# The gate products of a two-layer hybrid block: twelve weight tiles per layer as six folded pairs

## Chip, cores and metric
One core of a Trainium2 chip. The metric is the device time of one execution in microseconds (us); lower is better.

## The reference, cut to what matters
The model has 512 tokens, width 2048 and two layers. The stage that is changed is the last line of the loop, the product `x @ ple_gate_w[i]` (2048 x 2048) and the sigmoid gate around it:

```python
for i in range(DEPTH):                    # DEPTH = 2
    y = _even_layer(x, ...) if i % 2 == 0 else _conv_layer(x, ...)
    x = _layernorm(DEEPNORM_ALPHA * x + y, post_ln_g[i], post_ln_b[i])
    x = x + (p[i] @ ple_w[i]) * jax.nn.sigmoid(x @ ple_gate_w[i])
```

## The kernel before, in words
All activations stand transposed: 16 chunks (`KC`) of 128 channels by 512 tokens (`T`). `Y` holds x, `Z` holds the product `p @ ple_w`. A matrix product is made in three passes for precision: each operand is split into a rounded part and a rest (`a_hi`, `a_lo` for activations, `w_hi`, `w_lo` for weights), and TensorE adds hi x hi, hi x lo and lo x hi. A weight tile is 128 x 2048: 16 blocks of 128 x 128, which make one chunk of 128 output channels. So a tile costs 16 x 3 = 48 matmuls of 512 columns. All matmuls have one line, the helper `mm` (L745).

A tile passes through five hands. SyncE loads it into one of the two slots of `w_raw` (in `whole`, L519) when the slot's last tile has been split. ScalarE writes `w_hi` (`split`, L1231) once TensorE has finished the tile that used that slot before. VectorE writes `w_lo` as `w_raw` minus `w_hi` (`split`, L1705). TensorE multiplies (`gemm`), into the PSUM banks `G[0]` and `G[1]` in turn. ScalarE applies the sigmoid from the bank (L1592), VectorE multiplies by `Z` (L2368) and adds to `Y` (L2370), and GpSimd stores the finished chunk to DRAM (`store`, L659).

The gate stage of a layer (`W_GATE`, tiles 0 to 15) stands behind the layer norm. In that norm VectorE subtracts the mean (L2118) and multiplies by the deviation (L2122), ScalarE applies scale and bias (L1577) and makes `a_hi` of the chunk (L1235), and GpSimd makes `a_lo` (`x1_low`, L651). Tiles 0 and 1 run interleaved while those chunks arrive (`gemm_pair`, with tile 1 seven chunks behind), tiles 2 to 14 run one after another in `gemms` and `gemm`, and tile 15 is made in quarters (layer 0, where ScalarE and VectorE split the new x as its chunks pass) or by halves of the tokens (layer 1). In layer 0 the convolution's first two tiles follow, interleaved in the same way.

The output projection of each layer (`W_OUT`) already has a folded form, `folded_pair`: two tiles make a block of two by two with 6 chunk pairs, and the four block products of each pair of chunks and half of the tokens, eight in all, are replaced by seven from sums of weights (`t1` to `t4`) and sums of activations (`folds`). Its pieces are split at L1484 (ScalarE) and L2194 (VectorE), its sums of weights are made by DMAs that add, from GpSimd's queue (L626, L629), its sums of activations at L2159, L2162 and L2164 with the split at L1474 and L2185 (VectorE's first one of a fold also serves L2175), and its extra products are emptied from PSUM by L2203 and L2212 to L2222. Its piece of 6 chunks has 18 matmuls of 256 columns; the 4 chunks outside of the scheme are done as before, with 512 columns. Each engine runs its list in the order in which it is written; waits are on semaphores.

## Time and profile before

| | us |
|---|---|
| median of 3 runs | 2089.8 |
| lowest, highest | 2089.51, 2090.85 |
| the profiled execution, its own time | 2089.52 |
| its span (first to last instruction) | 2087.8 |
| TensorE matmul busy in the span | 2080.8 (100%) |
| VectorE, ScalarE, GpSimd busy | 1341.0, 872.9, 394.8 |
| chain that ended last: share of TensorE | 97% |
| mean granted TensorE clock | 1.000 |

A row of instructions gives line, engine, operation, what is written and read with partitions x elements, the count, then busy us and the mean ns of one, then the idle time of the engine just before and what ended it. Back-to-back instructions of one engine overlap by some tens of ns in the records, so the distance of two starts is what an instruction costs in a full queue. GpSimd is POOL, VectorE DVE, ScalarE ACT, TensorE PE.

### The profile page before, as it was taken

Reading aid. Unit: us, or ns where it says so; the run is one execution under the profiler, and the core shown is the slowest. Engines: PE = TensorE matmul, PEld = TensorE weight load, DVE = VectorE, ACT = ScalarE, POOL = GpSimd, SP = SyncE. Lnnn points to the kernel's source line nnn. Section 1 sums busy time; section 2 is a strip of 40 time slices with the busy share of each in tenths; the row PEclk is TensorE's granted clock in tenths of the full one; section 3 lists DMA queues with packets and bytes.
Section 4 is the critical chain, followed back from the end, with each engine's and each line's share of the span. In section 5 each row is a group of like instructions: output and inputs, shape, how many; then the busy total and the mean of one; then the engine's idle time right before and its main releaser. Section 6 shows DMA issues by size and latency. Waiting matters only on the chain.

```text
span 2087.8 us, 29899 instructions
## 1 busy us (share of the span) xinstructions
PE 2080.8 (100%) x11050; PEld 1749.4 (84%) x11050; DVE 1341.0 (64%) x2295; ACT 872.9 (42%) x1148; POOL 394.8 (19%) x232
## 2 busy tenths in 40 slices
PE   9999999999999999999999999999999999999999
PEld 7878888888888888898788888888888888997888
DVE  5235575665765747787733588888888986887332
ACT  4225465464654657354622322222323453447221
POOL 0000000000000004110400034444757521104000
PEclk9999999999999999999999999999999999999999
DMA  8322222212222122695333322222222235852431
GB/s 320 142 101 90 73 80 80 76 64 81 67 95 80 60 80 81 161 228 145 107 109 121 136 100 85 98 101 101 91 91 101 101 121 127 218 158 82 145 108 68
DMA packets 46947, 233.51 MB, mean 112 GB/s; under 512 B 5456, under 2 KB 5728, under 8 KB 26896
## 3 DMA queue, kind: packets, MB, share of 16 engines
q1 hardware_dynamic: 35424, 190.33, 26.4%
q0 software_dynamic: 10000, 36.36, 7.0%
q10 hardware_dynamic: 1440, 5.77, 0.9%
q8 instruction: 45, 0.74, 0.1%
q14 instruction: 38, 0.31, 0.0%
HBM read 224.05 MB, written 8.39 MB: 111 GB/s over the span
## 4 chain that ended last, share of the span: by engine, by line
PE 97%; DMA 1%; DVE 1%; ACT 1%; issue 0%; DVEq 0%; ACTq 0%
PE G L745 83%; PE X L745 8%; PE T L745 5%; DMA w_raw<-wall_in 1%; PE T L927 1%; DVE w_lo L2194 0%; PE T L1048 0%; ACT w_hi L1484 0%; ACT a_hi L1235 0%; ACT Z L1430 0%; ACT Y L1577 0%; PE T L1053 0%; PE T L899 0%; DVE Y L2229 0%; ACT L1322 0%
## 5 line engine op out<-in xcount | busy, mean ns | idle before, releaser
L745 PE MATMUL G<-a_hi,w_hi 128*128 128x512 f32 (+1 forms) x2524 | 980.0, 388 | 0.7 <-ACT a_hi L1235 0.6
L745 PE MATMUL G<-a_hi,w_lo 128*128 128x512 f32 (+1 forms) x2524 | 974.0, 386 | 0.0
L745 PE MATMUL G<-a_lo,w_hi 128*128 128x512 f32 (+1 forms) x2524 | 972.3, 386 | 0.0
L1231 ACT ACTIVATE w_hi<-w_raw 128x2048 fp32r<-128x2048 f32 x147 | 281.7, 1916 | 787.3 <-PE G L745 774.2
L1705 DVE TENSOR_TENSOR w_lo<-w_raw,w_hi 128x2048 fp32r<-128x2048 f32 x104 | 242.0, 2327 | 494.2 <-ACT w_hi L1231 494.2
L745 PEld LDWEIGHTS G<-a_hi,w_hi 128*128 128x128 f32 x2524 | 474.1, 188 | 99.4 <-ACT a_hi L1235 1.5
L745 PEld LDWEIGHTS G<-a_hi,w_lo 128*128 128x128 f32 x2524 | 474.1, 188 | 96.2 <-issue 0.2
L745 PEld LDWEIGHTS G<-a_lo,w_hi 128*128 128x128 f32 x2524 | 474.2, 188 | 94.5 <-issue 0.5
L2429 DVE SCALAR_TENSOR_TENSOR T<-tmp,par,T 128x512 f32<-128x512 f32 x464 | 306.9, 747 | 0.0
L687 POOL TENSOR_TENSOR w_lo<-w_raw,w_hi 128x2048 fp32r<-128x2048 f32 x45 | 207.8, 4618 | 232.4 <-ACT w_hi L1231 232.4
L1484 ACT ACTIVATE w_hi<-w_raw 128x768 fp32r<-128x768 f32 (+1 forms) x86 | 66.2, 783 | 89.7 <-PE G L745 27.1
L2194 DVE TENSOR_TENSOR w_lo<-w_raw,w_hi 128x768 fp32r<-128x768 f32 (+1 forms) x86 | 73.7, 880 | 38.3 <-ACT w_hi L1484 37.8
L671 POOL TENSOR_TENSOR a_lo<-Y,a_hi 128x512 fp32r<-128x512 f32 x15 | 21.3, 1456 | 339.6 <-DVE Z L1917 339.6
L666 POOL CAST v_lo<-Y 128x512 fp32r<-128x512 f32 x1 | 0.6, 609 | 385.3 <-PE X L745 385.3
L745 PE MATMUL T<-folds,w_hi 128*128 128x256 f32 x360 | 65.4, 283 | 0.0
L651 POOL TENSOR_TENSOR a_lo<-Y,a_hi 128x512 fp32r<-128x512 f32 x32 | 44.2, 1403 | 108.7 <-ACT a_hi L1235 108.4
L745 PEld LDWEIGHTS T<-folds,w_hi 128*128 128x128 f32 x360 | 56.4, 192 | 0.2
L745 PE MATMUL T<-folds,w_lo 128*128 128x256 f32 x180 | 50.9, 283 | 0.0
L2417 DVE TENSOR_TENSOR tmp<-G,tmp 128x512 f32<-128x512 f32 x16 | 11.0, 687 | 59.6 <-PE G L745 59.6
L1235 ACT ACTIVATE a_hi<-Y 128x512 fp32r<-128x512 f32 x80 | 46.0, 622 | 5.1 <-PE G L745 2.6
L1330 ACT ACTIVATE Z<-Z,nmx 128x128 f32<-128x128 f32 (+1 forms) x64 | 35.2, 552 | 20.8 <-DVE nmx L1990 20.7
L745 PE MATMUL G<-pk,w_hi 128*128 128x512 f32 x128 | 42.6, 413 | 0.5 <-ACT Z L1430 0.5
(336 smaller groups left out, 2246.9 us busy)
## 6 DMA issues: line engine op xcount, KB each, us to landing
w_raw<-wall_in SPq DMA_DIRECT2D x150, 1024.0 KB, 4.8
w_raw<-wall_in SPq DMA_DIRECT2D x42, 384.0 KB, 5.2
w_raw<-wall_in SPq DMA_DIRECT2D x36, 256.0 KB, 5.4
w_raw<-wall_in POOLq DMA_DIRECT2D x24, 384.0 KB, 5.5
Y<-w_in POOLq DMA_DIRECT2D x2, 2048.0 KB, 15.6
x_residual<-Y POOLq DMA_DIRECT2D x16, 256.0 KB, 3.7
out<-Y POOLq DMA_DIRECT2D x15, 256.0 KB, 3.6
Z<-xT_in SPq DMA_DIRECT2D x6, 512.0 KB, 9.4
```

The lines of the kernel that those rows point to most:

```text
L651: pool.tensor_tensor(a_lo[:, j, :], chunk(Y, j), a_hi[:, j, :].bitcast(F), ALU.subtract).then_inc(S("ops_split"), 1)
L671: pool.tensor_tensor(a_lo[:, c, :], chunk(Y, c), a_hi[:, c, :].bitcast(F), ALU.subtract).then_inc(S("ops_split"), 1)
L687: pool.tensor_tensor(w_lo[:, w.slot, :], w_raw[:, w.slot, :], w_hi[:, w.slot, :].bitcast(F), ALU.subtract).then_inc(S("w_split"), 1)
L745: return pe.matmul(o, l, r, start=start, stop=stop)
L927: last = pe.transpose(TB[at // T][:, at % T:at % T + P], prob_of(ti)[:, mj * P:(mj + 1) * P], ident)
L1231: f(w_hi[:, w.slot, :], w_raw[:, w.slot, :], ACT.Copy).then_inc(S("w_hi"), 1)
L1235: f(a_hi[:, j, :], chunk(Y, j), ACT.Copy).then_inc(S("ops_hi"), 1)
L1330: f(prob_of(ti), prob_of(ti), ACT.Exp, bias=nmx[:, o + ti:o + ti + 1], accum_out=rsum[:, o + ti:o + ti + 1]).then_inc(S("exps"), 1)
L1484: f(w_ring[0][ring_slot(p, name)][:, 0:piece_width(name)], source(p, name), ACT.Copy).then_inc(S("w_hi" if last else "piece_hi"), KC - 2 * ...
L1705: tt(w_lo[:, w.slot, :], w_raw[:, w.slot, :], w_hi[:, w.slot, :].bitcast(F), ALU.subtract).then_inc(S("w_split"), 1)
L2194: tt(w_ring[1][at][:, 0:n], source(p, name), w_ring[0][at][:, 0:n].bitcast(F), ALU.subtract).then_inc(S("w_split" if last else "piece_low" ...
L2429: stt(acc, src, cw, acc, op0=ALU.mult, op1=ALU.add).then_inc(S("tap"), 1)
```

## The change
Tiles 2 to 13 of each gate stage become six pairs. In a pair, chunks 0 to 2 and 3 to 5 are the two halves of the scheme (`GATE_K` = 3 chunk pairs) and chunks 6 to 15 are done as before: `r1` and `r2` are those ten blocks of the first and of the second tile (1280 wide, 512 columns), and `b11, t1, t3, t2, b22, b21, t4` are seven products of 3 blocks (384 wide, 256 columns). Tile 14 is done plainly from three pieces, tile 15 as before.

- Sums of weights: VectorE adds them (`add_weights`), in place or into `gate_sum` (in `tmp`).
- Sums of activations: VectorE makes three folds (`make_fold`) behind its last instruction of the layer norm, ScalarE and VectorE split them (`gate_fold_high`, `gate_fold_low`), and only then is the first piece of pair 1 split.
- `w_hi` and `w_lo` hold `r1`, `r2` and a ring of four places of 384; a piece is written when TensorE has done the fourth one before it.
- The products in `TB[0]`, `TB[1]` are emptied into `gate_pre` (the sum before the sigmoid, in `tmp`) in three steps between the last pieces' splits; the banks `X[1], X[2]` or `G[1], G[0]` are added behind (`add_bank`), and both chunks' sigmoids follow (`gate_sigmoid`).
- SyncE loads four pieces per pair in place of two tiles (640 KB and 384 KB of each tile). GpSimd's list is unchanged but for semaphore values.

The helpers that are left out below give semaphore values and places. The diff, with 12 spaces of indentation and empty lines taken out:

```diff
+GATE_K = 3
+GATE_QUAD = GATE_K * P
+GATE_REST = 2 * GATE_QUAD
+GATE_PAIRS = 6
+GATE_SMALL = ("b11", "t1", "t3", "t2", "b22", "b21", "t4")
+GATE_TILE = GATE_PAIRS + 1
+GATE_DONE = [(p, name) for p in range(1, GATE_TILE) for name in ("r1", "r2") + GATE_SMALL] + [
+    (GATE_TILE, name) for name in ("r1", "b11", "b21")]
+GATE_MADE = [(1, "r1")]
+for pair in range(1, GATE_TILE):
+    GATE_MADE += [(pair, name) for name in ("r2",) + GATE_SMALL[:4]] + [(pair + 1, "r1")]
+    GATE_MADE += [(pair, name) for name in GATE_SMALL[4:]]
+GATE_MADE += [(GATE_TILE, "b11"), (GATE_TILE, "b21")]
+N_GATE = len(GATE_MADE) - 1
+PIECES_BEFORE = (N_PIECES - 1, 2 * (N_PIECES - 1) + N_GATE)
...
+def gate_pieces(layer):
+    def load(p, tile, small):
+        at = slice(0, GATE_REST) if small else slice(GATE_REST, D)
+        sp.dma_start(w_raw[:, 1 - tile, at], wall[W_GATE[layer] + 2 * p + tile][:, at]).then_inc(
+            S(("b11_landed", "b22_landed")[tile] if small else "rest_landed"), 16)
+    sp.wait_ge(S("w_split"), W_GATE[layer] + 1)
+    load(1, 0, False)
+    load(1, 0, True)
+    sp.wait_ge(S("w_split"), W_GATE[layer] + 2)
+    load(1, 1, False)
+    load(1, 1, True)
+    for p in range(2, GATE_TILE + 1):
+        sp.wait_ge(*gate_low(layer, p - 1, "r1"))
+        load(p, 0, False)
+        if p < GATE_TILE:
+            sp.wait_ge(*gate_low(layer, p - 1, "r2"))
+            load(p, 1, False)
+            sp.wait_ge(*gate_low(layer, p - 1, "b22"))
+            load(p, 1, True)
+            sp.wait_ge(*gate_low(layer, p - 1, "b21"))
+            load(p, 0, True)
+    sp.wait_ge(*gate_low(layer, GATE_PAIRS, "b22"))
+    tile = W_GATE[layer] + KC - 1
+    sp.dma_start(w_raw[:, 0, :], wall[tile]).then_inc(S("w_landed0"), 16)
+    sp.wait_ge(*gate_low(layer, GATE_PAIRS, "b21"))
+    load(GATE_TILE, 0, True)
...
+def gate_products(layer, p, name, out, highs, lows, start, stop):
+    pe.wait_ge(*gate_low(layer, p, name))
+    hi, lo = gate_place(p, name)
+    n = len(highs)
+    for k in range(n):
+        at = slice(k * P, (k + 1) * P)
+        mm(out, hi[:, at], highs[k], start and k == 0, False)
+        mm(out, hi[:, at], lows[k], False, False)
+        last = mm(out, lo[:, at], highs[k], False, stop and k == n - 1)
+    return last
+def gate_pair(layer, p):
+    g = G_GATE[layer] + 2 * p
+    one, two = (X[1], X[2]) if p % 2 else (G[1], G[0])
+    first, second = TB[0][:, 0:HALF_T], TB[1]
+    if p > 1:
+        pe.wait_ge(*drained(Idx(g - 4)))
+        pe.wait_ge(*drained(Idx(g - 3)))
+    def tokens(chunks, half):
+        at = slice(half * HALF_T, (half + 1) * HALF_T)
+        return [a_hi[:, c, at] for c in chunks], [a_lo[:, c, at] for c in chunks]
+    def fold(s):
+        return [[gate_folds[k][:, s, n, :] for k in range(GATE_K)] for n in range(2)]
+    rest = range(2 * GATE_K, KC)
+    whole = [a_hi[:, c, :] for c in rest], [a_lo[:, c, :] for c in rest]
+    ones_at, twos_at = range(GATE_K), range(GATE_K, 2 * GATE_K)
+    done = S("piece_done")
+    gate_products(layer, p, "r1", one[:, :], *whole, True, False).then_inc(done, 1)
+    gate_products(layer, p, "r2", two[:, :], *whole, True, False).then_inc(done, 1)
+    if p > 1:
+        pe.wait_ge(*gate_emptied(layer, p - 1, 4))
+    else:
+        pe.wait_ge(S("fold_lo"), gate_fold(layer, GATE_K))
+    gate_products(layer, p, "b11", first, *tokens(ones_at, 0), True, True).then_inc(done, 1)
+    gate_products(layer, p, "t1", second[:, HALF_T:T], *fold(1), True, True).then_inc(done, 1)
+    gate_products(layer, p, "t3", second[:, 0:HALF_T], *fold(0), True, True).then_inc(done, 1)
+    pe.wait_ge(*gate_emptied(layer, p, 1))
+    gate_products(layer, p, "t2", first, *fold(2), True, True).then_inc(done, 1)
+    gate_products(layer, p, "b22", two[:, 0:HALF_T], *fold(3), False, True).then_inc(done, 1)
+    gate_products(layer, p, "b21", one[:, 0:HALF_T], *tokens(twos_at, 0), False, False).then_inc(done, 1)
+    gate_products(layer, p, "t4", one[:, HALF_T:T], *tokens(twos_at, 1), False, True).then_inc(
+        *((S("gemm_done"), 2 * GATE_PAIRS) if p == GATE_PAIRS else (done, 1)))
+def gate_tile(layer):
+    p, done = GATE_TILE, S("piece_done")
+    pe.wait_ge(*drained(Idx(G_GATE[layer] + 2 * p - 4)))
+    def whole(lo, hi):
+        return [a_hi[:, c, :] for c in range(lo, hi)], [a_lo[:, c, :] for c in range(lo, hi)]
+    gate_products(layer, p, "r1", X[1][:, :], *whole(2 * GATE_K, KC), True, False).then_inc(done, 1)
+    gate_products(layer, p, "b11", X[1][:, :], *whole(0, GATE_K), False, False).then_inc(done, 2)
+    gate_products(layer, p, "b21", X[1][:, :], *whole(GATE_K, 2 * GATE_K), False, True).then_inc(S("gemm_done"), 1)
...
-    gemms(w + 2, g + 2, KC - 4)
-    gemm(Idx(w + KC - 2), Idx(g + KC - 2))
+    for p in range(1, GATE_TILE):
+        gate_pair(layer, p)
+    gate_tile(layer)
...
+    def gate_fold_high(i):
+        act.wait_ge(S("fold_raw"), gate_fold(layer, i + 1))
+        if i == 2:
+            act.wait_ge(S("gemm_done"), W_PLE[layer][1] + 1)
+        f(gate_folds[i][:, :, 0, :], (gate_raw[1] if i else gate_raw[0]), ACT.Copy).then_inc(S("fold_hi"), 1)
+    def gate_piece_high(p, name):
+        if name[0] == "t":
+            act.wait_ge(*gate_after("centred", layer, 4 * (p - 1) + ("t1", "t3", "t2", "t4").index(name) + 1))
+        else:
+            act.wait_ge(*gate_landed(layer, p, name))
+        act.wait_ge(*gate_place_free(layer, p, name))
+        last = (p, name) == GATE_MADE[-1]
+        f(gate_place(p, name)[0], gate_source(p, name), ACT.Copy).then_inc(
+            S("w_hi" if last else "piece_hi"), 2 * GATE_PAIRS + 1 if last else 1)
+    def gate_sigmoid(p):
+        for n in range(2):
+            act.wait_ge(*drained(Idx(g + 2 * p + n)))
+            pre = gate_pre[:, n * T:(n + 1) * T]
+            f(pre, pre, ACT.Sigmoid).then_inc(S("squared"), 1)
+    for i in range(GATE_K):
+        gate_fold_high(i)
+    gate_piece_high(1, "r1")
+    gate(Idx(w), Idx(g), 0)
+    gate_piece_high(1, "r2")
+    gate(Idx(w + 1), Idx(g + 1), 0)
+    for p, name in GATE_MADE[2:]:
+        if name == "b11" and p > 1:
+            gate_sigmoid(p - 1)
+        gate_piece_high(p, name)
     gate_end = W_GATE[layer] + KC
+    split(Idx(gate_end - 1))
+    act.wait_ge(S("x_out"), KC * layer + KC - 2)
+    act.wait_ge(S("gemm_done"), gate_end - 1)
+    frees(f(ln_sq[1], X[1][:, :], ACT.Sigmoid), Idx(g + KC - 2))
...
-    with dve.Fori(0, KC // 2 - 1) as i:
-        for k in range(2):
-            split(Idx(w + 2 + k, 2, i))
-            gate(Idx(g + k, 2, i), i * 2 + k, i * 2 + (layer * KC + k + 1))
+    def make_fold(i):
+        n = gate_fold(layer, i)
+        dve.wait_ge(S("x1_ready"), layer * KC + GATE_K + i + 1)
+        if i == 2:
+            dve.wait_ge(S("fold_lo"), n)
+        raw = gate_raw[1] if i else gate_raw[0]
+        tt(raw[:, 0:2, :], Y4[:, i, :, :], Y4[:, i:GATE_K + i + 1:GATE_K, 1, :], ALU.subtract).then_inc(S("fold_step"), 1)
+        dve.wait_ge(S("fold_step"), 2 * n + 1)
+        tt(raw[:, 2, :], raw[:, 1, :], Y4[:, i, 0, :], ALU.subtract).then_inc(S("fold_step"), 1)
+        dve.wait_ge(S("fold_step"), 2 * n + 2)
+        tt(raw[:, 3, :], raw[:, 2, :], Y4[:, GATE_K + i, 0, :], ALU.add).then_inc(S("fold_raw"), 1)
+    def gate_fold_low(i):
+        dve.wait_ge(S("fold_hi"), gate_fold(layer, i + 1))
+        dve.wait_ge(S("fold_raw"), gate_fold(layer, i + 1))
+        tt(gate_folds[i][:, :, 1, :], (gate_raw[1] if i else gate_raw[0]), gate_folds[i][:, :, 0, :].bitcast(F),
+           ALU.subtract).then_inc(S("fold_lo"), 1)
+    def add_weights(p, name, dst, a, b):
+        dve.wait_ge(*gate_landed(layer, p, "b11"))
+        dve.wait_ge(*gate_landed(layer, p, "b22"))
+        n = 4 * (p - 1) + ("t1", "t3", "t2", "t4").index(name)
+        dve.wait_ge(*gate_after("centred", layer, n))
+        tt(dst, a, b, ALU.add).then_inc(S("centred"), 1)
+    def gate_piece_low(p, name):
+        dve.wait_ge(*gate_high(layer, p, name))
+        hi, lo = gate_place(p, name)
+        last = (p, name) == GATE_MADE[-1]
+        tt(lo, gate_source(p, name), hi.bitcast(F), ALU.subtract).then_inc(
+            S("w_split" if last else "piece_low"), 2 * GATE_PAIRS + 1 if last else 1)
+    def gate_lows(p, *names):
+        for name in names:
+            gate_piece_low(p, name)
+    one_right, two_left, two_right = [gate_pre[:, n * HALF_T:(n + 1) * HALF_T] for n in range(1, 4)]
+    def empty_one(p):
+        dve.wait_ge(*gate_done(layer, p, "b11"))
+        dve.tensor_copy(gate_pre[:, 0:HALF_T], TB[0][:, 0:HALF_T]).then_inc(S("fold_emptied"), 1)
+    def empty_two(p):
+        dve.wait_ge(*gate_done(layer, p, "t3"))
+        dve.tensor_copy(gate_pre[:, HALF_T:3 * HALF_T], TB[1][:, :]).then_inc(S("fold_emptied"), 1)
+        dve.wait_ge(*gate_emptied(layer, p, 2))
+        tt(two_right, two_left, TB[1][:, 0:HALF_T], ALU.subtract).then_inc(S("fold_emptied"), 1)
+    def empty_three(p):
+        dve.wait_ge(*gate_done(layer, p, "t2"))
+        dve.wait_ge(*gate_emptied(layer, p, 3))
+        tt(fold_sum, gate_pre[:, 0:HALF_T], TB[0][:, 0:HALF_T], ALU.add).then_inc(S("fold_emptied"), 1)
+        dve.wait_ge(*gate_emptied(layer, p, 4))
+        tt(one_right, one_right, fold_sum, ALU.add).then_inc(S("fold_emptied"), 1)
+        two = gate_pre[:, T:2 * T].rearrange("p (h t) -> p h t", h=2)
+        tt(two, two, fold_sum.unsqueeze(1).broadcast_to([P, 2, HALF_T]), ALU.subtract).then_inc(S("fold_emptied"), 1)
+        dve.wait_ge(*gate_emptied(layer, p, 6))
+    def add_bank(p, n):
+        dve.wait_ge(*gate_done(layer, p, ("t4", "b22")[n]))
+        bank = ((X[1], X[2]) if p % 2 else (G[1], G[0]))[n]
+        pre = gate_pre[:, n * T:(n + 1) * T]
+        frees(tt(pre, pre, bank[:, :], ALU.add), Idx(g + 2 * p + n))
+    def gate_two(p):
+        for n in range(2):
+            j = 2 * p + n
+            dve.wait_ge(*gate_after("squared", layer, 2 * (p - 1) + n + 1))
+            pre = gate_pre[:, n * T:(n + 1) * T]
+            tt(pre, pre, chunk(Z, j), ALU.mult).then_inc(S("ple_gated"), 1)
+            dve.wait_ge(S("ple_gated"), layer * KC + j + 1)
+            tt(chunk(Y, j), chunk(Y, j), pre, ALU.add).then_inc(S("x_out"), 1)
+    make_fold(0)
+    make_fold(1)
+    gate_fold_low(0)
+    gate_fold_low(1)
+    make_fold(2)
+    gate_fold_low(2)
+    for p in range(1, GATE_TILE):
+        b12, b22, b21 = [gate_source(p, name) for name in ("t3", "b22", "b21")]
+        if p == 1:
+            gate_lows(p, "r1")
+            gate(Idx(g), 0, layer * KC + 1)
+            gate_lows(p, "r2")
+            gate(Idx(g + 1), 1, layer * KC + 2)
+        else:
+            add_bank(p - 1, 0)
+            gate_lows(p, "r2")
+            gate_two(p - 1)
+        add_weights(p, "t1", gate_sum, gate_source(p, "b11"), b12)
+        add_weights(p, "t3", b12, b12, b22)
+        gate_lows(p, "b11", "t1")
+        add_weights(p, "t2", gate_sum, gate_sum, b22)
+        gate_lows(p, "t3", "t2")
+        add_weights(p, "t4", gate_sum, gate_sum, b21)
+        gate_lows(p + 1, "r1")
+        empty_one(p)
+        gate_lows(p, "b22")
+        empty_two(p)
+        gate_lows(p, "b21")
+        empty_three(p)
+        gate_lows(p, "t4")
+        add_bank(p, 1)
+    add_bank(GATE_PAIRS, 0)
+    gate_lows(GATE_TILE, "b11", "b21")
+    gate_two(GATE_PAIRS)
+    split(Idx(w + KC - 1))
     if w + KC < W_TILES:
         split(Idx(w + KC))
-    gate(Idx(g + KC - 2), KC - 2, layer * KC + KC - 1)
+    bank = Idx(g + KC - 2)
+    dve.wait_ge(*drained(bank))
+    tt(ln_sq[1], ln_sq[1], chunk(Z, KC - 2), ALU.mult).then_inc(S("ple_gated"), 1)
+    dve.wait_ge(S("ple_gated"), layer * KC + KC - 1)
+    tt(chunk(Y, KC - 2), chunk(Y, KC - 2), ln_sq[1], ALU.add).then_inc(S("x_out"), 1)
     if layer == 0:
         for j in range(12):
             low(OPS_CONV, j, chunk(Y, j))
```

## Rows read from the trace of the kernel before

**Rows 1.** The page: busy time by engine, then two stretches of 10.88 and 20.58 us.

```profile
PE 2080.8 (100%) x11050; PEld 1749.4 (84%) x11050; DVE 1341.0 (64%) x2295; ACT 872.9 (42%) x1148; POOL 394.8 (19%) x232
...
1046.09:1056.97 10.88, 10.88 (x49) 9.01 (x48) 3.58 (x3) 2.40 (x2) 0.54 (x1) 1.00 0.37 120
902.72:923.30 20.58, 20.58 (x152) 19.62 (x151) 19.60 (x31) 11.29 (x15) 3.41 (x4) 1.00 0.94 233
```

**Rows 2.** Timeline, all engines, where an output pair's `b11` ends (start us, us, engine).

```profile
910.18 0.40 PE L745 MATMUL T<-folds,w_hi 128*128 128x256 f32 x2
910.38 0.42 DVE L2203 COPY fold_sum<-T 128x256 f32<-128x256 f32 x1 [0.26 <-PE T L745]
```

**Rows 3.** Timeline of VectorE, emptying an output pair's products.

```profile
920.39 0.41 DVE L2219 TENSOR_TENSOR fold_sum<-fold_sum,T 128x256 f32<-128x256 f32 x1
920.84 0.42 DVE L2221 TENSOR_TENSOR Y<-Y,fold_sum 128x256 f32<-128x256 f32 x1
921.18 0.68 DVE L2222 TENSOR_TENSOR Y<-Y,fold_sum 128x512 f32<-128x512 f32 x1
921.97 0.69 DVE L2229 TENSOR_TENSOR Y<-Y,X 128x512 f32<-128x512 f32 x1
```

**Rows 4.** Timeline of VectorE, start of a fold in layer 0.

```profile
855.40 0.69 DVE L2159 TENSOR_TENSOR tmp<-Y 128x512 f32<-128x512 f32 x1
856.13 0.42 DVE L2162 TENSOR_TENSOR tmp<-tmp,Y 128x256 f32<-128x256 f32 x1
```

**Rows 5.** Groups by form: splits of 768 weights, of folds (VectorE and ScalarE).

```profile
L2194 DVE TENSOR_TENSOR w_lo<-w_raw,w_hi 128x768 fp32r<-128x768 f32 x62 | 58.4, 954 | 34.2 <-ACT w_hi L1484 34.1
L2185 DVE TENSOR_TENSOR folds<-tmp,folds 128x1024 fp32r<-128x1024 f32 x12 | 14.6, 1219 | 0.0
L1474 ACT ACTIVATE folds<-tmp 128x1024 fp32r<-128x1024 f32 x12 | 12.7, 1056 | 21.9 <-DVE tmp L2164 21.9
```

**Rows 6.** Timeline, all engines, where TensorE waited for a piece's `w_lo`.

```profile
876.08 0.96 DVE L2194 TENSOR_TENSOR w_lo<-w_raw,w_hi 128x768 fp32r<-128x768 f32 x1 [2.21 <-ACT w_hi L1484]
...
876.63 0.28 PE L745 MATMUL X<-folds,w_lo 128*128 128x256 f32 x1
...
877.09 0.39 PE L745 MATMUL X<-a_hi,w_hi 128*128 128x256 f32 x1 [0.19 <-DVE w_lo L2194]
877.32 0.28 PE L745 MATMUL X<-a_lo,w_hi 128*128 128x256 f32 x1
```

**Rows 7.** Timelines, start of the gate stage, layer 0: VectorE, ScalarE, GpSimd, TensorE.

```profile
1021.59 1.87 DVE L2122 TENSOR_TENSOR Y<-Y,X 128x512 f32<-128x512 f32 x3
...
1025.57 1.14 ACT L1235 ACTIVATE a_hi<-Y 128x512 fp32r<-128x512 f32 x2
...
1020.13 8.81 POOL L651 TENSOR_TENSOR a_lo<-Y,a_hi 128x512 fp32r<-128x512 f32 x7 [0.58 <-ACT a_hi L1235]
...
1028.87 0.63 PE L745 MATMUL G<-a_lo,w_hi 128*128 128x512 f32 x2
1035.01 0.39 PE L745 MATMUL G<-a_hi,w_hi 128*128 128x512 f32 x1
```

**Rows 8.** Timelines of GpSimd and of VectorE, convolution stage.

```profile
1660.11 4.62 POOL L687 TENSOR_TENSOR w_lo<-w_raw,w_hi 128x2048 fp32r<-128x2048 f32 x1 [4.34 <-ACT w_hi L1231]
...
1661.24 4.03 DVE L2475 TENSOR_TENSOR Y<-Y,Z 128x512 f32<-128x512 f32 x1 [0.27 <-ACT Y L1684]
```

**Rows 9.** Timelines of GpSimd (two of 15 alike, here one) and of VectorE, output stage.

```profile
819.48 3.33 POOL L671 TENSOR_TENSOR a_lo<-Y,a_hi 128x512 fp32r<-128x512 f32 x1
...
818.26 3.40 DVE L1705 TENSOR_TENSOR w_lo<-w_raw,w_hi 128x2048 fp32r<-128x2048 f32 x1 [2.19 <-ACT w_hi L1231]
```

**Rows 10.** Timelines, convolution's first tiles: VectorE's split of the second, TensorE.

```profile
1190.75 2.28 DVE L1705 TENSOR_TENSOR w_lo<-w_raw,w_hi 128x2048 fp32r<-128x2048 f32 x1
...
1193.23 0.39 PE L745 MATMUL G<-a_hi,w_hi 128*128 128x512 f32 x1
```

**Rows 11.** The page: DMA issues, KB each and median us to landing.

```profile
w_raw<-wall_in SPq DMA_DIRECT2D x42, 384.0 KB, 5.2
```

More of the change, by code:

```diff
@@ L415, in landed @@
             in_pieces = (FOLD_TO + 1 - FOLD_FROM) * len([n for n in W_OUT if w.base > n + 2 * FOLD_TO])
+            in_pieces += (GATE_TILE if w.slot else GATE_PAIRS) * len([n for n in W_GATE if w.base > n + 2 * GATE_TILE])
             return S(f"w_landed{w.slot}"), w.half(1 - in_pieces) * 16
@@ L475, in after, with gate_after, gate_high @@
         def after(name, n, steps):
-            return S(name), steps + LN_COUNTS[name] * n
+            return S(name), steps + LN_COUNTS[name] * n + (GATE_COUNTS.get(name, 0) if n else 0)
+        def gate_after(name, layer, steps):
+            return S(name), steps + LN_COUNTS[name] * (2 * layer + 1) + GATE_COUNTS[name] * layer
+        def gate_high(layer, p, name):
+            n = GATE_MADE.index((p, name)) + 1
+            if n == len(GATE_MADE):
+                return S("w_hi"), W_GATE[layer] + 2 * GATE_TILE + 1
+            return S("piece_hi"), PIECES_BEFORE[layer] + n
@@ new lines, in gate_width, with gate_place @@
+        def gate_width(name):
+            return D - GATE_REST if name[0] == "r" else GATE_QUAD
+        def gate_place(p, name):
+            if name[0] == "r":
+                at = D if name == "r1" else 0
+            elif p == GATE_TILE:
+                at = GATE_RING[("b11", "b21").index(name)]
+            else:
+                at = GATE_RING[(7 * (p - 1) + GATE_SMALL.index(name)) % 4]
+            return [w.rearrange("p s n -> p (s n)")[:, at:at + gate_width(name)] for w in (w_hi, w_lo)]
@@ new lines, in gate_place_free @@
+        def gate_place_free(layer, p, name):
+            if name[0] == "r":
+                return gate_done(layer, p - 1, name) if p > 1 else (S("gemm_done"), W_GATE[layer] + int(name[1]))
+            if p == GATE_TILE:
+                return gate_done(layer, p - 1, {"b11": "b21", "b21": "t4"}[name])
+            n = 7 * (p - 1) + GATE_SMALL.index(name) - 4
+            if n < 0:
+                return S("gemm_done"), W_GATE[layer] + (1 if n < -2 else 2)
+            return gate_done(layer, n // 7 + 1, GATE_SMALL[n % 7])
@@ new lines, in gate_source, with gate_landed @@
+        def gate_source(p, name):
+            if name[0] == "r":
+                return w_raw[:, 1 if name == "r1" else 0, GATE_REST:D]
+            if name in ("t1", "t2", "t4"):
+                return gate_sum
+            slot, at = {"b11": (1, 0), "b21": (1, GATE_QUAD), "t3": (0, 0), "b22": (0, GATE_QUAD)}[name]
+            return w_raw[:, slot, at:at + GATE_QUAD]
+        def gate_landed(layer, p, name):
+            if name[0] == "r":
+                n = (2 * (N_FOLDS + 1) + 2 * GATE_PAIRS + 1) * layer + 2 * (N_FOLDS + 1) + min(2 * p, 2 * GATE_PAIRS + 1)
+                return S("rest_landed"), 16 * n
+            if name in ("b12", "b22", "t3"):
+                return S("b22_landed"), 16 * ((N_FOLDS + 1) * (layer + 1) + GATE_PAIRS * layer + p)
+            return S("b11_landed"), 16 * ((N_FOLDS + 1) * (layer + 1) + GATE_TILE * layer + p)
@@ L479, in quarter, with gate_emptied, gate_fold @@
+        def gate_emptied(layer, p, step):
+            return S("fold_emptied"), 8 * N_FOLDS * (layer + 1) + 6 * (GATE_PAIRS * layer + p - 1) + step
+        def gate_fold(layer, i):
+            return PAIR_K * (layer + 1) + GATE_K * layer + i
         def quarter(q):
@@ L1594, in second_part @@
                 w, g = W_GATE[layer], G_GATE[layer]
-                for j in range(2):
-                    split(Idx(w + j + 2))
-                    gate(Idx(w + j), Idx(g + j), 0)
-                with act.Fori(1, KC // 2 - 1) as i:
-                    for k in range(2):
-                        split(Idx(w + 2 + k, 2, i))
-                        gate(Idx(w + k, 2, i), Idx(g + k, 2, i), i * 2 + (k - 1))
+                def gate_fold_high(i):
[3 more added lines that the diff above has]
+                    f(gate_folds[i][:, :, 0, :], (gate_raw[1] if i else gate_raw[0]), ACT.Copy).then_inc(S("fold_hi"), 1)
@@ L2154, in fold @@
                         dve.wait_ge(S("gated"), second + 1)
[L2155 removed]
+                    n = layer * (PAIR_K + GATE_K) + i
                     if i >= 2:
```

52 lines of the change are left out of this document (35 added, 17 removed).

## The prediction

> **What bounds the kernel now.** First the busy times on the profile's page: TensorE is busy for 2080.8 us of a span of 2087.8, VectorE for 1341.0 [rows 1]. So only two things can move the end: what TensorE itself is given to do, and any wait that is put in front of it. Then two stretches of that section. A plain gate tile takes 10.88 us for 48 matmuls of 512 columns, all of it TensorE, with VectorE busy for 3.58: 0.2267 us per matmul, and 21.76 us per two tiles. A folded pair of the output projection takes 20.58 us for 24 matmuls of 512 columns and 126 of 256; taking off 24 x 0.2267 leaves 0.120 per matmul of 256 columns, a little over half. In that pair VectorE is busy for 19.60 of 20.58 us and still hides [rows 1].
>
> **What TensorE gets.** Per pair and pass set, r1 and r2 keep 10 blocks each: 60 matmuls x 0.2267 = 13.60 us. The seven products have 7 x 9 = 63 matmuls x 0.120 = 7.56 us, 1.08 per product. Together 21.16 against 21.76: 0.60 us saved per pair, 7.2 us in twelve pairs, if nothing waits. Tile 14 in three pieces still has 48 wide matmuls, 10.88 us. The gain per pair is small because six chunks give up 36 wide matmuls (8.16 us) for 7.56.
>
> **The tail of each pair.** The pieces are short: VectorE must now empty three products and split three weight pieces while TensorE runs b11 to b21, 1.08 us each. I count from the end of b11; then t3 ends at 2.16, t2 at 3.24, and TensorE wants b22 at 3.24, b21 at 4.32, t4 at 5.40. Prices: VectorE starts 0.20 after a product's end (910.18 to 910.38) [rows 2]. One start to the next costs 0.34 at 256 columns, 0.44 if it waits for the one before, and 0.79 behind a 512-wide one that is waited for [rows 3]; 0.73 by the fold's first step [rows 4]. A split of 384 has no row: between 256 (0.42 busy) [rows 3] and 768 (0.95) [rows 5] a line gives 0.555 busy, 0.47 start to start; the ends of the interval would shift the result by at most 0.13 each way per split. TensorE starts 0.05 after the split's end, 1.01 after its start at 768 [rows 6], so 0.61 after its start at 384, and the first matmuls behind a wait cost 0.10 more (the second starts 0.23 after the first, not 0.12) [rows 6].
> The list: empty_one at 0.20; b22's split by 0.9, in time. empty_two waits for t3: copy at 2.36, the subtraction at 3.09, b21's split at 3.43, ready at 4.04, in time by 0.28. empty_three then stands in front of t4's split: 3.90, 4.34, 4.68 and, since it waits for its own last result, t4's split only at 5.47. TensorE gets t4 at 6.08, 0.68 late, and with 0.10 for the restart a pair loses 0.78. So it costs 21.94 us: **0.60 saved, 0.78 lost, +0.17 us per pair, +2.0 for twelve.** Behind t4 nobody else waits for it: add_bank, r2's split, two gates (2.8 us), four sums of weights and five splits take VectorE to about 18.6, and the next b11 ends at 21.94, so the delay does not pile up. Those sums and splits cost nothing as long as these 3 us are left; if that cover goes, each 0.47 us is 0.47 us of TensorE.
>
> **Loads.** Each pair has four loads for two. The pieces b11 and b21 of the next pair are asked for at about 4.0, when b21 is split; such a load lands in 5.2 us [rows 11], at 9.3, and VectorE first adds them at 12.2. SyncE's wait for b22 and b21 stands in front of the loads of the next r1 and r2, wanted only at 17. At the end tile 15's megabyte is asked for ahead of tile 14's b11, which is wanted 14 us behind. GpSimd only stores here, two chunks at a time. I cost these at nothing.
>
> **The start of each gate stage**, twice. Before, VectorE ends the layer norm at 1023.39 (1021.59 and three steps of 0.60), ScalarE makes the last a_hi by 1026.71, and TensorE goes from tiles 0, 1 to tile 2 at 1035.01 [rows 7]. Now three folds stand between the norm and the first piece. Alone, a fold is 0.73 + 0.46 + 0.34 = 1.5 us [rows 3, 4], its high part 1.06 on ScalarE and its low part 1.22 [rows 5]. The third reuses the second's place, so it runs in series: low parts of the first two from 1027.8 to 1030.1, third fold to 1031.7, its high to 1032.8, its low to 1034.0. r1's high runs beside that (1280 wide, about 1.3, above the 1.06 for 1024), and its low (0.95 + 512 columns at 1.04 ns, the slope of that line, = 1.48) ends at 1035.6: TensorE starts 0.64 late, 0.74 with the restart.
> But GpSimd makes a_lo of chunks 9 to 15 in this very time, seven of 1.26 us in a row from 1020.13 to 1028.94 [rows 7]. Two rows show what that does. A VectorE product of two SBUF tensors, of 0.68 us otherwise, took 4.03 from 1661.24 and ended at 1665.27, 0.54 behind a GpSimd split that ended at 1664.73 [rows 8]. And a VectorE split of two SBUF tensors that began at 818.26 amid GpSimd's a_lo took 3.40 where 2.28 is usual [rows 10], while the GpSimd instruction at 819.48 ended 3.33 us later, 1.15 behind it [rows 9]: they take turns, whole instructions at a time. The norm's instructions beside it read one PSUM bank and keep 0.68 us.
> With turns: fold 1 ends its steps at 1024.44, 1025.87, 1027.30, fold 2 at 1028.99, 1030.42, 1030.88; a_lo of chunks 12 to 15 ends at 1025.59, 1027.02, 1028.45 and 1030.14 (1028.94 before). TensorE wants the last one at about 1029.1 [rows 7] and stands for 1.1, so it wants r1 at 1036.2. From 1030.88 the serial part runs free: lows of folds 1 and 2 to 1033.2 (the second's high at 1032.0), fold 3 to 1034.9, its high to 1036.0, its low to 1037.2, r1's low to 1038.75, TensorE at 1038.8, with the restart 1038.9 in place of 1035.01: **+3.85 us per layer, +7.7.** In layer 1 the same lines stand at the same distances.
> The Trainium skill ("SBUF — State Buffer", Who interferes with whom) says that a VectorE instruction with two SBUF inputs and a GpSimd instruction that reads SBUF exclude each other for the whole instruction. By that rule this part of the sum is the 7.7 us; by the plain durations without it, 1.5. This trace agrees with it in the 4.03 us instruction.
>
> **The end of layer 0's stage.** ScalarE now does tile 14's sigmoid (0.6 busy, 0.50 in the queue) before, not behind, the high part of the convolution's first tile. VectorE is full from there to the second tile's split, which began at 1190.75 and ended at 1193.03; TensorE used it at 1193.23 [rows 10]. 0.50 later it is 0.36 late, 0.46 with the restart. It is between 0 and 0.6; I take **+0.46.**
>
> **Sum:** 2.0 + 7.7 + 0.46 = +10.2 us. The profiled execution took 2089.52 (span 2087.8), so it would be 2099.7; the median of the runs is 0.3 above it, so I forecast **2100.0**. About 0.2%, 4.2 us, can be told from no change.
>
> **Rivals.**
> The port costs nothing: VectorE's small folds slip between GpSimd's, and the start costs 0.74 per layer. Then 2089.8 + 2.0 + 1.5 + 0.46 = 2093.8, just inside 0.2%. For it: no row has a 512- or 256-wide fold beside a_lo. Against: both rows of two SBUF inputs that meet GpSimd waited. 10%.
> The turns go worse. If GpSimd finishes all its a_lo first, folds begin at 1028.94 and r1 comes at 1039.8, +4.8 per layer; if VectorE keeps the port through back-to-back folds and lows, a_lo of chunk 15 ends near 1035.5 and TensorE loses 6.4 per layer. With the rest that is 2101.9 to 2105.1. 12%.
> The steady part has one more late thing: b21 has only 0.28 to spare, and if its split is 0.3 late in each pair too, 3.6 us come on top: 2103.6. 10%.
> The other side: VectorE keeps up with the tail, so TensorE gets its 0.60 in every pair. It decides at one point, t4's split, which must start by 4.79 and not 5.47. If also the start takes only its 0.74, the sum is -7.2 + 1.5 + 0.46: 2084.6, faster. For it: VectorE has 3 us to spare per pair. Against: even without any wait for its own results (0.60, 0.34, 0.47, 0.34, 0.34, 0.60 from 2.36) the split starts at 5.05. 5%. The tail alone kept up, with the start as forecast, gives 2090.8: 3%.
> That the change doesn't do what it says I leave out: the products and their order stand in the code.
>
> **Numbers.** My case 60%, the others 10, 12, 10, 5 and 3. Within 0.2%: 10 + 3 = 13%. Faster: 5%. Slower: 82%. The range takes in the free port at its low end and the worse turns at its high end, with the bound of 0.13 per split: 2093.5 to 2106.
>
> **What would show it.** In a pair of the gate stage: TensorE idle before t4's first matmul by 0.6 to 0.7 us, released by VectorE's split of the weights, and nowhere else; a period of 21.9 us. VectorE's third step of emptying between b21's and t4's splits. At the start of the stage: fold steps of 1.5 us or more where 0.68 and 0.42 would do, beside GpSimd's a_lo, some of these above 1.26; TensorE waiting about 1.1 us for a_lo and about 2.6 for r1. I am wrong if the period is 21.2 (tail hidden), if folds keep their plain durations, or if TensorE waits for a load, a sigmoid or b21.

## The result, and the profile after

The changed kernel takes **2102.16 us** (median of 5 runs, 2100.61 to 2102.47); the kernel before, timed beside it, 2090.85 (5 runs, 2089.51 to 2091.3). The ratio is 1.0056, with a 95% interval of 1.0042 to 1.0069: 11.3 us slower. The profiled execution took 2102.47 us, 2100.6 of it span.

The page's busy times of the changed kernel, which answer to the first row of [rows 1]:

```profile
span 2100.6 us, 30734 instructions
...
PE 2080.3 (99%) x11374; PEld 1761.2 (84%) x11374; DVE 1462.1 (70%) x2551; ACT 906.4 (43%) x1242; POOL 397.4 (19%) x232
```

TensorE has 324 instructions more and is busy for as long as before (2080.8); the span grew by 12.8. That reads as if nothing were saved, but each wait of TensorE puts some busy time beside its idle time: a 256-wide matmul's record lasts 0.28 where the next one usually starts 0.12 behind it, and the first one behind a wait lasts 0.39. So the waits have to be counted one by one. The view of waits of the changed kernel, TensorE over the whole span (line waited for, us in total, times, longest):

```profile
PE X L877 <- DVE w_lo L2629: 7.7, 8, 2.4
PE G L877 <- DVE w_lo L2629: 2.9, 6, 0.5
PE G L877 <- POOL a_lo L783: 2.0, 2, 1.0
```

L2629 is VectorE's split of a gate piece. Of its 14 waits twelve are of 0.49 us, one per pair (six in bank `G`, six in `X`), and two of 2.4 us, one at the start of each gate stage. The third row is GpSimd's `a_lo` at the same two starts.

**The tail of a pair.** VectorE, the changed kernel, from the end of pair 2's `b11` (1078.18, 0.20 before the first row); it answers to [rows 3]:

```profile
1078.38 0.42 DVE L2642 COPY tmp<-T 128x256 f32<-128x256 f32 x1 [4.14 <-PE T L877]
...
1080.52 0.69 DVE L2646 COPY tmp<-T 128x512 f32<-128x512 f32 x1 [0.96 <-PE T L877]
1081.25 0.42 DVE L2648 TENSOR_TENSOR tmp<-tmp,T 128x256 f32<-128x256 f32 x1
1081.59 0.55 DVE L2629 TENSOR_TENSOR w_lo<-w_raw,w_hi 128x384 fp32r<-128x384 f32 x1
1082.06 0.41 DVE L2653 TENSOR_TENSOR fold_sum<-tmp,T 128x256 f32<-128x256 f32 x1
1082.50 0.42 DVE L2655 TENSOR_TENSOR tmp<-tmp,fold_sum 128x256 f32<-128x256 f32 x1
1082.85 0.68 DVE L2657 TENSOR_TENSOR tmp<-tmp,fold_sum 128x512 f32<-128x512 f32 x1
1083.57 0.56 DVE L2629 TENSOR_TENSOR w_lo<-tmp,w_hi 128x384 fp32r<-128x384 f32 x1
```

And TensorE there, which answers to [rows 6]:

```profile
1083.41 0.28 PE L877 MATMUL G<-a_hi,w_lo 128*128 128x256 f32 x1
1084.18 0.39 PE L877 MATMUL G<-a_hi,w_hi 128*128 128x256 f32 x1 [0.49 <-DVE w_lo L2629]
1084.40 0.28 PE L877 MATMUL G<-a_lo,w_hi 128*128 128x256 f32 x1
```

The three instructions of `empty_three` (L2653 to L2657) stand between b21's split and t4's. t4's split starts 5.39 behind the end of b11, TensorE gets t4 at 6.00, and the next matmul comes 0.22 behind it instead of 0.12. From one pair to the next it is 21.85 to 21.88 us, in five distances of each layer.

**The start of the stage.** VectorE, GpSimd and TensorE of the changed kernel in layer 0, in that order; they answer to [rows 7] and, by their durations, to [rows 4]:

```profile
1024.44 1.11 DVE L2603 TENSOR_TENSOR tmp<-Y 128x512 f32<-128x512 f32 x1
1025.59 1.40 DVE L2605 TENSOR_TENSOR tmp<-tmp,Y 128x256 f32<-128x256 f32 x1
1027.03 1.40 DVE L2607 TENSOR_TENSOR tmp<-tmp,Y 128x256 f32<-128x256 f32 x1
1028.35 1.78 DVE L2603 TENSOR_TENSOR tmp<-Y 128x512 f32<-128x512 f32 x1
1030.17 1.37 DVE L2605 TENSOR_TENSOR tmp<-tmp,Y 128x256 f32<-128x256 f32 x1
1031.58 0.42 DVE L2607 TENSOR_TENSOR tmp<-tmp,Y 128x256 f32<-128x256 f32 x1
...
1037.20 1.23 DVE L2613 TENSOR_TENSOR pk<-tmp,pk 128x1024 fp32r<-128x1024 f32 x1 [1.13 <-ACT pk L1793]
1038.36 1.49 DVE L2629 TENSOR_TENSOR w_lo<-w_raw,w_hi 128x1280 fp32r<-128x1280 f32 x1
...
1021.19 10.07 POOL L783 TENSOR_TENSOR a_lo<-Y,a_hi 128x512 fp32r<-128x512 f32 x7 [0.58 <-ACT a_hi L1428]
...
1013.99 0.50 PE L877 MATMUL G<-a_hi,w_hi 128*128 128x512 f32 x1
...
1031.31 0.50 PE L877 MATMUL G<-a_lo,w_hi 128*128 128x512 f32 x1 [1.00 <-POOL a_lo L783]
...
1039.90 0.50 PE L877 MATMUL X<-a_hi,w_hi 128*128 128x512 f32 x1 [2.39 <-DVE w_lo L2629]
```

Steps of a fold that take 0.69 and 0.42 alone take 1.11 to 1.78 while GpSimd works, and the sixth, behind GpSimd's last, takes 0.42 again. GpSimd's seven need 10.07 us for 8.81. TensorE then waits twice. From the first `a_hi` matmul of tile 0 to r1 it is 25.91 us (1013.99 to 1039.90); in the kernel before the same matmul stood at 1012.95 and the next tile came 22.06 later, at 1035.01 [rows 7]. So the start lost 3.85 us, and 0.11 more with the restart behind r1's first matmul. In layer 1 the distance is 25.94.

**Something of another kind** follows. Windows of the changed kernel (us, busy times of TensorE, its weight load, VectorE, ScalarE, GpSimd, then the granted clock, the DMA share and GB/s), right behind r1's first matmuls and in the next pair:

```profile
1041.56:1044.54 2.98, 2.98 (x8) 2.30 (x7) 2.94 (x5) 0.73 (x2) 0.60 (x1) 0.50 0.79 275
1063.64:1085.51 21.87, 21.38 (x125) 18.82 (x124) 15.18 (x25) 7.05 (x11) 1.08 (x2) 1.00 0.37 122
```

For some 3.4 us the granted clock was 0.50, the 1.2 GHz level, and matmuls stood 0.43 apart instead of 0.23. From r1's first matmul to b11's it is 15.34 us here and 13.73 in layer 1, where the clock stayed at 1.00: 1.6 us lost.

**The end of layer 0's stage.** VectorE starts the split of the convolution's second tile at 1198.51, and TensorE waits 0.19 for it and restarts; in all 0.35 + 0.11 = 0.46 us ([rows 10] had none):

```profile
1198.51 2.29 DVE L1927 TENSOR_TENSOR w_lo<-w_raw,w_hi 128x2048 fp32r<-128x2048 f32 x1
...
1200.85 0.50 PE L877 MATMUL G<-a_hi,w_hi 128*128 128x512 f32 x1 [0.19 <-DVE w_lo L1927]
```

The account of the span's 12.8 us: two starts 2 x 3.96 = 7.9; twelve pairs 12 x (21.87 - 21.76) = 1.3; the end of the stage 0.46; the low clock 1.6; together 11.3. The other 1.5 lies outside of what was changed: 1.2 is already there in the first 30 us, ahead of anything that was changed, and other executions differ by as much there (the same matmul of tile 0 stands between 1012.8 and 1015.4 in the nine profiles of this case).

### The profile page after: what moved, and what is told of

It is laid out like the page before. It is cut to its first block, busy times and chain, and to the rows that moved or that the text cites. A ratio compares the mean times of both kernels' runs of the same rounds, so it can differ in the third digit from the quotient of the medians.

```text
span 2100.6 us, 30734 instructions
## 1 busy us (share of the span) xinstructions
PE 2080.3 (99%) x11374; PEld 1761.2 (84%) x11374; DVE 1462.1 (70%) x2551; ACT 906.4 (43%) x1242; POOL 397.4 (19%) x232
## 4 chain that ended last, share of the span: by engine, by line
PE 90%; DVE 5%; DMA 2%; ACT 2%; issue 1%; SPq 0%; POOL 0%; DVEq 0%; ACTq 0%
PE G L877 69%; PE X L877 13%; PE T L877 7%; DMA w_raw<-wall_in 2%; PE T L1059 1%; DVE w_lo L2629 0%; DVE w_lo L1927 0%; DVE tmp L2646 0%; DVE tmp L2657 0%; DMA tmp<-masks_in 0%; DVE a_lo L1932 0%; DVE Y L2344 0%; DVE tmp L2603 0%; DVE tmp L2605 0%; DVE w_lo L2416 0%
## 5 line engine op out<-in xcount | busy, mean ns | idle before, releaser
L877 PE MATMUL G<-a_hi,w_hi 128*128 128x512 f32 (+1 forms) x2264 | 876.5, 387 | 4.1 <-DVE w_lo L2629 2.9
L877 PE MATMUL G<-a_lo,w_hi 128*128 128x512 f32 (+1 forms) x2264 | 868.4, 384 | 2.0 <-POOL a_lo L783 2.0
L877 PE MATMUL G<-a_hi,w_lo 128*128 128x512 f32 (+1 forms) x2264 | 869.7, 384 | 0.0
L1927 DVE TENSOR_TENSOR w_lo<-w_raw,w_hi 128x2048 fp32r<-128x2048 f32 x78 | 182.5, 2340 | 300.8 <-ACT w_hi L1424 300.8
L877 PE MATMUL X<-a_hi,w_hi 128*128 128x512 f32 (+1 forms) x308 | 110.6, 359 | 8.8 <-DVE w_lo L2629 7.7
L877 PE MATMUL X<-a_lo,w_hi 128*128 128x512 f32 (+1 forms) x308 | 109.1, 354 | 0.0
L877 PE MATMUL X<-a_hi,w_lo 128*128 128x512 f32 (+1 forms) x308 | 109.1, 354 | 0.0
L1802 ACT ACTIVATE w_hi<-w_raw 128x384 fp32r<-128x384 f32 (+1 forms) x78 | 59.7, 768 | 79.7 <-PE T L877 76.6
L877 PEld LDWEIGHTS X<-a_hi,w_hi 128*128 128x128 f32 x308 | 58.6, 190 | 19.3 <-DVE w_lo L2629 9.7
L2629 DVE TENSOR_TENSOR w_lo<-w_raw,w_hi 128x384 fp32r<-128x384 f32 (+1 forms) x78 | 67.4, 866 | 8.5 <-ACT w_hi L1802 7.2
```

Of the source, the lines that this page charges most:

```text
L877: return pe.matmul(o, l, r, start=start, stop=stop)
L1802: f(gate_place(p, name)[0], gate_source(p, name), ACT.Copy).then_inc(S("w_hi" if last else "piece_hi"), 2 * GATE_PAIRS + 1 if last else 1)
L1927: tt(w_lo[:, w.slot, :], w_raw[:, w.slot, :], w_hi[:, w.slot, :].bitcast(F), ALU.subtract).then_inc(S("w_split"), 1)
L2629: tt(lo, gate_source(p, name), hi.bitcast(F), ALU.subtract).then_inc(S("w_split" if last else "piece_low"), 2 * GATE_PAIRS + 1 if last else 1)
```

## The experiments

Theory: the loss is (a) t4's split behind `empty_three`, 0.75 us of TensorE per pair, (b) VectorE and GpSimd taking turns at the start of the stage, some 3 us per layer, with (c) a short serial part of the folds, 0.7 per layer, and (d) the sigmoid in front of the convolution's split. Rivals: that the folds are late by their number alone, whatever GpSimd does; that the turns only shift waits that would be there anyway; that another wait takes the place of a removed one. The kernel before, timed beside four of the kernels (the changed one again, t4's split first, almost no `a_lo`, folds late and spread), took 2090.31 us (27 runs); beside the other three, 2090.0 (12 runs).

**The changed kernel again.** No edit.

> The changed kernel once more, unchanged, for one look. Two things of its profiled execution may belong to the execution and not to the kernel: a delay of 1.1 us before the heads (at about 60 us), and the granted clock of 0.50 for 3.4 us behind TensorE's wait of 2.4 us at the first gate stage, which cost some 1.5 us. My theory (the change costs about 10 us by itself: 3.8 us at each start, 0.11 us in each pair, 0.5 at the convolution) expects the pairs' period of 21.87 us and both waits at the starts again, and the delay at 60 us gone or different. If the drop of the clock is caused by the wait, it comes again in at least one of the layers; if it is chance, it does not.

Measured: 2100.91 us in one execution, span 2099.0. The three rows of waits are the same to the tenth, the period is 21.87, and the granted clock stays at 1.00 behind both waits of 2.4 us. So the waits belong to the kernel. That the clock stayed up in both layers speaks for chance by the test set here; the profiles below show that it is not chance alone.

**t4's split first.**

```diff
                     gate_lows(p, "b21")
-                    empty_three(p)
                     gate_lows(p, "t4")
+                    empty_three(p)
```

> Only edit: VectorE splits t4's weights before the third step of emptying, not behind it. Theory (that order is the only late thing in a pair): the split can start about 1.5 us earlier than TensorE wants it minus its own length, TensorE does not wait inside a pair, the period falls from 21.87 to 21.16 to 21.2 us, and twelve pairs give back 8.0 to 8.5 us: ratio to the kernel before about 1.001 to 1.002, 3 to 4 us above it by the median. Rival (products of 256 columns cost more here than in the output stage, or another wait stands right behind, b21 or the next pair's emptying): the period stays above 21.5 and less than 5 us come back.

Measured: 2093.98 us (11 runs, 2091.49 to 2100.53), ratio to the kernel before 1.0018 [1.0009, 1.0027]. TensorE waits for L2629 twice in all, and the distance of pairs is 21.12 or 21.13. The waits of this kernel:

```profile
PE X L877 <- DVE w_lo L2629: 4.8, 2, 2.4
PE G L877 <- POOL a_lo L783: 2.1, 2, 1.0
```

Both twelves are gone and nothing came in their place: (a) is shown, with 21.87 - 21.12 = 0.75 us per pair, 9.0 in all. The median is 8.2 below that of the changed kernel; in this kernel's profile the clock fell behind both waits of 2.4 us, which gives back part.

**Almost no `a_lo` on GpSimd.** GpSimd writes 16 of the 512 columns of `a_lo` for chunks 9 to 15, and the rest is left out, so the third pass of those chunks is not computed with its values.

```diff
-                    pool.tensor_tensor(a_lo[:, j, :], chunk(Y, j), a_hi[:, j, :].bitcast(F), ALU.subtract).then_inc(
+                    n = T if j < 9 else 16
+                    pool.tensor_tensor(a_lo[:, j, 0:n], chunk(Y, j)[:, 0:n], a_hi[:, j, 0:n].bitcast(F), ALU.subtract).then_inc(
```

> GpSimd makes only 16 of 512 columns of a_lo for chunks 9 to 15 of the gate stages; the rest of that a_lo keeps old values, so this part of the products is left out, with as many instructions and waits as before. Theory (VectorE's folds and GpSimd's a_lo take turns at one port): the fold steps keep their plain 0.7 and 0.4 us, TensorE does not wait for a_lo, and waits for r1 by 0.6 us where it was 2.4: each start costs 0.7 to 0.8 us where it was 3.8, so 6 us come back in all. Rival (the start is the serial chain of folds over two engines alone, and GpSimd only happens beside it): the fold steps of 1.1 to 1.8 us stay, and under 2 us come back.

Measured: 2093.3 us (10 runs, 2092.88 to 2094.49), ratio 1.0015 [1.0006, 1.0024]. VectorE's folds and TensorE of this kernel (lines one higher):

```profile
1023.27 0.68 DVE L2604 TENSOR_TENSOR tmp<-Y 128x512 f32<-128x512 f32 x1
1023.98 0.42 DVE L2606 TENSOR_TENSOR tmp<-tmp,Y 128x256 f32<-128x256 f32 x1
1024.44 0.43 DVE L2608 TENSOR_TENSOR tmp<-tmp,Y 128x256 f32<-128x256 f32 x1
...
1035.49 0.50 PE L878 MATMUL X<-a_hi,w_hi 128*128 128x512 f32 x1 [0.46 <-DVE w_lo L2630]
```

The same instructions on VectorE, and each at its plain duration. No wait for `a_lo` is left, and r1 comes 22.67 behind the first matmul of tile 0 (1012.82): 0.61 late, 0.72 with the restart, which is (c). The other 3.24 of the 3.96 per layer is (b), and the rival that the number of folds is enough falls. The median is 8.9 below the changed kernel's, where the two starts account for 6.5; in this profile the clock also stayed at 1.00, and a fall costs 1.6. The Trainium skill ("SBUF — State Buffer", Who interferes with whom) states that a VectorE instruction with two inputs in SBUF and a GpSimd instruction that reads SBUF contend, and calls what they share an exclusive lock; the two timelines agree, by 1.40 against 0.42 us for the same step.

**Folds behind `a_lo`, nothing else moved.** The wait is on the semaphore of GpSimd's last `a_lo`.

```diff
+                dve.wait_ge(*ops_split(OPS_GATE[layer], KC))
                 make_fold(0)
```

> Only edit: VectorE waits for all of GpSimd's a_lo before it makes the first fold; r1 of pair 1 stays behind all folds. Theory (two causes at the start, the port and the serial folds in front of r1): the fold steps have their plain 0.7 and 0.4 us, GpSimd's seven a_lo take 8.8 us, TensorE doesn't wait for a_lo, and waits for r1 by about 4.7 us in one piece: the start costs 4.8 us, 1 us more than in the changed kernel, some 2 us in both layers. Rival (the port alone was the cost): without overlap the start costs less than the 3.8 us of the changed kernel.

Measured: 2105.82 us (4 runs, 2105.41 to 2106.15), ratio 1.007 [1.0049, 1.009]. VectorE and TensorE:

```profile
1029.41 0.69 DVE L2603 TENSOR_TENSOR tmp<-Y 128x512 f32<-128x512 f32 x1 [5.53 <-POOL a_lo L783]
1030.13 0.42 DVE L2605 TENSOR_TENSOR tmp<-tmp,Y 128x256 f32<-128x256 f32 x1
...
1040.44 0.80 PE L877 MATMUL X<-a_hi,w_hi 128*128 128x512 f32 x1 [4.84 <-DVE w_lo L2629]
1041.04 0.63 PE L877 MATMUL X<-a_lo,w_hi 128*128 128x512 f32 x1
```

The turns are gone and so is the wait for `a_lo`, and the kernel is slower still: r1 comes 27.09 behind tile 0's first matmul (1013.35), 5.03 late. So taking turns is not by itself the loss. VectorE loses 4.4 us to GpSimd (the first five steps take 7.14 us from start to start, and 2.70 here), but waiting loses more. The other candidate is that everything between the norm and r1 stands in one queue, and the next experiment changes that. Here the granted clock was at 0.50 behind the wait in both layers, in layer 0 already when r1's first matmul began and in layer 1 from 0.19 us into it.

**Folds late and spread.** VectorE waits for the last `a_lo`, makes two folds, and then splits r1 before it does any fold's low part; the third fold goes behind r2's split. ScalarE's list is interleaved in the same way.

```diff
+                dve.wait_ge(*ops_split(OPS_GATE[layer], KC))
                 make_fold(0)
                 make_fold(1)
-                gate_fold_low(0)
-                gate_fold_low(1)
-                make_fold(2)
-                gate_fold_low(2)
...
                         gate_lows(p, "r1")
-                        gate(Idx(g), 0, layer * KC + 1)
+                        gate_fold_low(0)
+                        gate_fold_low(1)
                         gate_lows(p, "r2")
+                        make_fold(2)
+                        gate(Idx(g), 0, layer * KC + 1)
+                        gate_fold_low(2)
```

> Folds behind GpSimd's a_lo and partly behind the first piece: VectorE begins them when all a_lo are made, splits r1 of pair 1 between the first two folds' steps and their low parts, and makes the third fold behind r2. Nothing is left out. Theory: GpSimd's a_lo keeps 1.26 us each, r1's low part is there before TensorE wants it, and the folds are there before b11 of pair 1, 13.6 us later; both starts cost nothing, 7.6 us come back and in the first layer also what the low clock cost, if that follows the wait: ratio about 1.001. Rival (VectorE has too much to do before b11 of pair 1, 18 us of work): TensorE waits before b11 or t1 instead, and under 5 us come back.

Measured: 2092.95 us (11 runs, 2089.95 to 2093.44), ratio 1.0012 [1.0003, 1.0021]. The waits:

```profile
PE G L877 <- DVE w_lo L2631: 2.9, 6, 0.5
PE X L877 <- DVE w_lo L2631: 2.9, 6, 0.5
```

Of the waits in the gate stages only the twelve tails are left. r1 needs no fold, TensorE wants no fold before the products, 13.6 us later, and VectorE has the time then. With the experiment before, which has the same wait, this shows the place of the loss: the order of the queue, not the work in it. The new order without the wait for `a_lo` was not run, so what the wait itself is worth in that order is not shown.

**The convolution's split before the sigmoid.** ScalarE:

```diff
                 split(Idx(gate_end - 1))
+                if gate_end < W_TILES:
+                    split(Idx(gate_end))
                 act.wait_ge(S("x_out"), KC * layer + KC - 2)
...
-                if gate_end < W_TILES:
-                    split(Idx(gate_end))
```

> Only edit: at the end of the gate stage of layer 0 ScalarE makes the high part of the convolution's first tile before tile 14's sigmoid, as the kernel before did. Theory: VectorE's queue starts 0.5 us earlier, TensorE no longer waits for the convolution's second tile, and 0.45 us come back: too little for the times to tell, so the profile decides: the wait of 0.35 us for a 2048-wide split of VectorE behind the gate stage is gone. Rival (the wait has another cause, such as the lows of the activations): it stays.

Measured: 2102.12 us (5 runs, 2098.84 to 2103.53), ratio 1.0042 [1.0022, 1.0062]. The time can't tell 0.46 us, the trace can: the matmuls across that place stand 0.23 apart.

```profile
1200.99 0.39 PE L877 MATMUL G<-a_lo,w_hi 128*128 128x512 f32 x1
1201.22 0.39 PE L877 MATMUL G<-a_hi,w_hi 128*128 128x512 f32 x1
1201.45 0.39 PE L877 MATMUL G<-a_hi,w_lo 128*128 128x512 f32 x1
```

In this profile the clock fell behind both waits of 2.4 us, so its span (2101.7) is no shorter.

**All three orders together.** The three edits above (t4 first, folds late and spread, the convolution's split first), nothing left out.

> The three edits together: t4's split before the third step of emptying, the folds behind GpSimd's a_lo and partly behind the first piece, and at the end of the stage the high part of the convolution's first tile before tile 14's sigmoid. Nothing is left out. Theory (the three costs are independent and cover all that the change costs): twelve pairs save 0.60 us each and nothing waits, so the kernel is 7 us faster than the one before: ratio 0.9965 to 0.9970, 2083 us. Rival (VectorE's queue, now fuller in front of b11 of pair 1, gives part of it back): TensorE waits before b11, t1 or the next r1, and the ratio is above 0.998.

Measured: **2082.53 us** (6 runs, 2080.95 to 2084.37), ratio to the kernel before 0.996 [0.9945, 0.9976]: 7.5 us faster than the kernel before, and 19.6 faster than the changed one. All six executions lie below the shortest of the kernel before in any comparison (2088.71). No wait of TensorE in the gate stage is left. The busy times on its page:

```profile
PE 2072.9 (100%) x11374; PEld 1758.5 (85%) x11374; DVE 1453.3 (70%) x2551; ACT 906.9 (44%) x1242; POOL 394.9 (19%) x232
```

The window of its first pair, from `b11` to the next `b11` (columns as above):

```profile
1049.25:1070.38 21.13, 21.13 (x125) 18.77 (x123) 15.77 (x26) 7.06 (x11) 1.08 (x2) 1.00 0.37 125
```

VectorE at its start of the stage, where r1's split comes between the folds and their low parts:

```profile
1030.32 0.43 DVE L2607 TENSOR_TENSOR tmp<-tmp,Y 128x256 f32<-128x256 f32 x1
...
1033.49 1.49 DVE L2631 TENSOR_TENSOR w_lo<-w_raw,w_hi 128x1280 fp32r<-128x1280 f32 x1 [0.77 <-ACT w_hi L1802]
1034.90 2.35 DVE L2615 TENSOR_TENSOR gate_folds<-tmp,gate_folds 128x1024 fp32r<-128x1024 f32 x2
```

r1 comes 22.10 behind tile 0's first matmul (22.06 before the change), and a pair takes 21.13 for 21.76: 12 x 0.63 = 7.6 us, which is the gain that was measured. TensorE's busy time is 7.9 under that of before. The mathematics gives what it should; the order of two queues had taken it away.

## Why the prediction was right

The forecast was 2100.0 (2093.5 to 2106) and slower; it is 2102.16, and 2100.61 to 2100.91 in the executions of the changed kernel whose mean clock is 1.000. The forecast was added to 2089.8; beside the changed kernel the kernel before took 2090.85, which is 1.05 of the 2.16 us between forecast and result. Point by point:

**What TensorE gets**: 21.16 forecast per pair, 21.12 to 21.13 measured where nothing waits (t4 first; all three). The saving is 0.63, not 0.60.

**The tail**: the mechanism and its place were right, t4's split behind `empty_three` and nowhere else; b21 was in time, with the split at 3.41 (forecast 3.43). The size was a little off: t4's split started at 5.39 and not at 5.47. The step that was too dear is the wait for its own last result, 0.79 behind a 512-wide instruction, taken from [rows 3]; it measured 0.72, the value that [rows 4] has for such a case. With the cheaper matmuls the pair takes 21.87 instead of 21.94: 1.3 us for twelve and not 2.0 (the forecast's own 0.78 - 0.60 would be 0.18 per pair, 2.2 in all). The rival that b21 is late too falls; that VectorE keeps up holds only if the queue is changed.

**Loads**: no wait of TensorE for a piece's load appears. Costed at nothing, rightly.

**The start**: forecast ends of the six first fold steps were 24.44, 25.87, 27.30, 28.99, 30.42 and 30.88 (and 1000); measured, less the 1.05 by which this execution's norm ended later, 24.50, 25.94, 27.38, 29.08, 30.49 and 30.95. The wait for `a_lo` was forecast as 1.1 and is 1.00, that for r1 as 2.6 and is 2.39; the row counts from the last matmul's recorded end, so both are some 0.15 longer in distances of starts. Forecast +3.85 per layer with the restart (its own times, 1038.9 less 1035.01, would give 3.89), measured 3.96. The part without the turns was forecast as 0.74 and measured, with `a_lo` nearly gone, as 0.72. The rival of a free port falls with that experiment. The rival that GpSimd finishes first was priced at +4.8 per layer; made on purpose, it cost 5.03.

**The end of layer 0's stage**: +0.46, measured 0.46.

**What the sum missed**: the granted clock of 0.50 behind the wait of 2.4 us, 1.6 us each time it happens. By terms the sum was 10.2, and the same terms measured 7.9 + 1.3 + 0.46 = 9.7; one fall of the clock brings it to 11.3, beside 11.3 between the medians. The tail that was 0.7 too dear offsets part of the clock that was left out, so the total is nearer than the terms, and that part is luck. The trace of before had no wait of TensorE of that length to read it from.
